# Weight halves moved by 16 to 64 bytes against the other SBUF tensors

## The reference

```python
def _sq_relu_mlp(h, w1, w2):
    a = jax.nn.relu(h @ w1)
    return (a * a) @ w2
```

## Time and profile before

| | us |
|---|---|
| median of 3 runs | 1690.45 |
| lowest and highest | 1687.62, 1692.09 |
| the profiled execution | 1686.52 |
| its span, first to last instruction | 1684.7 |
| TensorE busy | 1643.3 (98%) |
| VectorE busy | 941.8 (56%) |
| ACT busy | 764.6 (45%) |
| POOL busy | 631.6 (37%) |

### The profile page before, as it was taken

One profiled execution on the slowest core, in us unless ns is written; L12 is line 12 of the kernel. 1 busy time (PEld: TensorE's weight loads), 2 busy tenths in 40 slices (PEclk: granted clock), 3 DMA queues, 4 the chain that ended last, 5 costly groups with the idle time before them and its releaser, 6 DMA issues. The chain is left out here.

```text
span 1684.7 us, 26528 instructions
## 1 busy us (share of the span) xinstructions
PE 1643.3 (98%) x10010; PEld 1410.8 (84%) x10010; DVE 941.8 (56%) x1657; ACT 764.6 (45%) x1326; POOL 631.6 (37%) x439
## 2 busy tenths in 40 slices
PE   6999999999999999999999999999999999999998
PEld 4987777788888889989987788798888888989896
DVE  6226566544445249848546664777545576555552
ACT  5324554532223245476545655444445434535351
POOL 1027767342220186643013332965200227323242
PEclk9999999999999999999999999999999999999998
DMA  8322122133333222245632110224411222222221
GB/s 326 128 74 69 56 75 80 54 140 125 120 111 118 100 100 101 101 175 200 238 121 67 51 51 29 97 101 172 178 51 51 101 100 100 101 100 100 100 101 50
DMA packets 29802, 181.68 MB, mean 108 GB/s; under 512 B 3352, under 2 KB 5784, under 8 KB 10112
## 3 DMA queue, kind: packets, MB, share of 16 engines
q1 hardware_dynamic: 22136, 150.12, 24.8%
q10 hardware_dynamic: 7560, 30.09, 5.0%
HBM read 169.57 MB, written 10.50 MB: 107 GB/s over the span
## 5 line engine op out<-in xcount | busy, mean ns | idle before, releaser
L438 PE MATMUL acc<-rarena,wh 128*128 128x512 f32 (+1 forms) x1720 | 650.9, 378 | 6.8 <-ACT farena L1613 1.3
L440 PE MATMUL acc<-rarena,wl 128*128 128x512 f32 (+1 forms) x1720 | 634.6, 369 | 0.0
L439 PE MATMUL acc<-rarena,wh 128*128 128x512 f32 (+1 forms) x1720 | 634.6, 369 | 0.0
L438 PEld LDWEIGHTS acc<-rarena,wh 128*128 128x128 f32 x1720 | 324.1, 188 | 81.3 <-issue 23.5
L440 PEld LDWEIGHTS acc<-rarena,wl 128*128 128x128 f32 x1720 | 324.1, 188 | 55.7
L439 PEld LDWEIGHTS acc<-rarena,wh 128*128 128x128 f32 x1720 | 324.5, 189 | 49.6 <-issue 0.5
L320 DVE TENSOR_TENSOR wl<-raw,wh 128x2048 fp32r<-128x2048 f32 x81 | 198.7, 2453 | 237.2 <-ACT wh L314 237.1
L314 ACT ACTIVATE wh<-raw 128x2048 fp32r<-128x2048 f32 x99 | 188.9, 1908 | 73.1 <-PE acc L440 66.5
L320 POOL TENSOR_TENSOR wl<-raw,wh 128x2048 fp32r<-128x2048 f32 x18 | 82.6, 4588 | 149.3 <-ACT wh L314 149.3
L2555 POOL TENSOR_TENSOR wl<-raw,wh 128x512 fp32r<-128x512 f32 x78 | 104.9, 1372 | 86.6 <-ACT wh L1330 86.4
L516 PE MATMUL acc<-wh,rarena 128*128 128x256 f32 x336 | 95.5, 284 | 2.2 <-DVE rarena L1792 2.1
(11 more groups left out here) (346 smaller groups left out, 3084.0 us busy)
## 6 DMA issues: line engine op xcount, KB each, us to landing
raw<-in_w SPq DMA_DIRECT2D x129, 1024.0 KB, 4.8
early<-in_wmod SPq DMA_DIRECT2D x8, 1024.0 KB, 19.7
farena<-in_gate ACTq DMA_DIRECT2D x4, 1024.0 KB, 4.9
mkv_scratch<-rarena ACTq DMA_DIRECT2D x2, 2048.0 KB, 11.9
rarena<-mkv_scratch ACTq DMA_DIRECT2D x1, 4096.0 KB, 14.4
farena<-in_rpb ACTq DMA_DIRECT2D x16, 240.0 KB, 3.6
farena<-in_x_grid SPq DMA_DIRECT2D x2, 1024.0 KB, 6.3
o_scratch<-early ACTq DMA_DIRECT2D x8, 256.0 KB, 2.0
```

Source lines behind the costliest of these rows:

```text
L438: mm(o, w[0], m[0], start=start, stop=False)
L439: mm(o, w[0], m[1], start=False, stop=False)
L440: return mm(o, w[1], m[0], start=False, stop=stop)
```

## The change

The tensors for the two weight halves become 64 words (256 bytes) longer, and the views on them that the kernel uses start some words in. `phased(name, p0, p1)` places the half for even jobs `p0` bytes and that for odd jobs `p1` bytes from the tensor's start (plus a multiple of 128 for the second). The scratch for DMA descriptors is cut from 16,384 to 64 bytes, which moves every later tensor and makes room. Shapes, order and instructions stay.

```diff
         raw = sb("raw", [128, 2, KT, JW])
-        wh = sb("wh", [128, 2, KT, JW], f32r)
-        wl = sb("wl", [128, 2, KT, JW], f32r)
+        def phased(name, p0, p1):
+            words = ctx.enter_context(nc.sbuf_tensor(name, [128, 2 * KT * JW + 64], f32r))
+            q = KT * JW + (p1 - p0) // 4
+            return words[:, p0 // 4:p0 // 4 + 2 * q].rearrange("p (s q) -> p s q", s=2)[:, :, 0:KT * JW]\
+                .rearrange("p s (k n) -> p s k n", k=KT)
+
+        wh = phased("wh", 16, 32)
+        wl = phased("wl", 48, 64)
...
-    nc = bacc.Bacc("TRN2", target_bir_lowering=False, num_devices=1)
+    nc = bacc.Bacc("TRN2", target_bir_lowering=False, num_devices=1, dynamic_dma_scratch_size=64)
```

## The result

The median of five runs is 1701.92 us (1698.38 to 1704.70) against 1690.41 for the kernel before; the ratio is 1.0075, with a 95% interval from 1.0062 to 1.0088. The forecast was no change.

The account below looks back on a forecast made before the run. The prediction took TensorE's stream of matmuls to bound the kernel; pitch, splits, transfers and scratch each added nothing, 0 us on 1686.5, so a median of 1690 (1687 to 1694 if unchanged), overall range 1665 to 1702.

Parts of the forecast that it names:

- What bounds the kernel: Whole kernel: the stream of matmuls sets the end, TensorE busy 1643.3 of 1684.7 us.
- The pitch: Distance of matmul starts, 226.6 ns at 512 columns and 120.0 at 256; bounds 86 us gained to 23 lost, taken as 0.
- The 13.3 ns: Time of each matmul over its columns, the same at both widths; 6792 matmuls, 90 us in all.
- The first reason: Weights and moving columns slip 3.65 times round 128 bytes per load, so displacement hardly changes how often they meet; 0 us.
- The second reason: 256-column groups average 283 or 284 ns whichever tensors are read, so the 13.3 ns do not depend on that; 0 us.
- The third reason: Other readers and writers of the same tensors, such as DVE, leave no mark on TensorE's steps (227 against 225 ns); 0 us.
- The splits, the transfers, the scratch: Weight splits on ACT and DVE and transfers into raw stay hidden by 6.6 us cover, scratch idle; cost nothing.
- straddling: Slower rival: displaced loads touch five blocks of 128 bytes instead of four, 3.3 ns each, 23 us, 1713; chance 0.11.
- The collision rival: Faster rival: the 13.3 ns are a phase-dependent collision of read streams; one round spared 1666 (0.12), wholly or mostly gone 1604 to 1650 (0.05).

Follow-up runs that it names:

- the control: The changed kernel with all four displacements at 0, scratch still cut and tensors still longer; ratio 0.9998 to the kernel before.
- the map: Kernel of matmul bursts alone, displacement stepped through 256 bytes; with advancing columns none under 226.6 ns at 512 columns, least 113.3 at 256.

## Why the prediction was wrong

- *What bounds the kernel*: right. Of the 13.7 us 13.3 lie in the pitch of the stream of matmuls.
- *The pitch, "between them I take nothing"*: this is the step that failed. The 13.3 ns at 512 columns went to 17.8 and 20.0 in the two kinds of jobs, 4152 matmuls dearer by 4.4 ns on the average (17.5 us over 4010 distances); I had 0. At 256 columns they shrank, by 1.1 ns with weights from the halves and by 1.9 with the halves moving; no case of mine had a loss at one width and a gain at the other.
- *The first reason, the slip of 3.65 rounds*: it counts meetings as if their number made the price. The runs show several settled pitches instead, such as 226.7, 231.1 and 233.3, and 113.3, 117.8 and 120.0. The displacement and the start decide which one, so where the streams meet has a price, whatever the number of meetings.
- *The second reason, equal means whatever is read*: the rows were right and said nothing, since all those groups have the same displacement, 0. I had written that no row shows another phase, and should have left it there.
- *The third reason*: other engines leave no mark, true before and after, but they are not TensorE's own two streams. SBUF — State Buffer of the Trainium skill ("Who interferes with whom") gives TensorE two independent read ports, for moving operand and weights, and I read no change out of that too. The runs do not bear that reading out: in bursts with nothing else at work the places of the two operands change the pitch by 6.7 ns (226.7 to 233.3).
- *The splits, the transfers, the scratch*: right, the control costs nothing (0.9998).
- *The rivals*: straddling had the sign and twice the size (23 us, measured 11.5), but not the cause: the control has every operand off a multiple of 128 and runs as before. The collision rival asked for a gain by any displacement; at 512 columns no place of the map was better than 0 bytes.

What in the chip keeps the rhythm was not settled. Shown is that the time is there when the columns advance through more than four places of 4 bytes, that smaller loads and loads from one place change the pitch without removing the time, and that the displacement and the start pick its value.

## What to carry to other kernels

Where matmuls run back to back, work out the pitch over the columns for each width; if it is the same everywhere, that can be one settled state out of several, and the places of the operands against each other are a setting to measure, per width, in short bursts (here within 256 bytes). A burst must be started in several ways before its number is carried over: one that has two stable pitches can fall on the other in the kernel. And evidence from rows that all share the setting in question is no evidence about changing it.

## What the runs showed of the hardware

- Weights displaced against the columns often cost 6.7 ns a matmul at 512 columns (226.7 to 233.3) and gain up to 6.7 at 256 (120.0 to 113.3), each 16 cycles at 2.4 GHz. Single places of the map are worse: 236.1 at 212 bytes and 512 columns, 122.3 at 108 bytes and 256 columns. In the bursts the displacements 0 and 256 bytes settle alike (226.7, 120.0); 128 does not (233.5 at 512).
- One displacement can have two pitches, and the start picks: 16 bytes at 512 columns had 226.7 in 4 starts and 233.3 in 11.
- An operand whose columns all come from one place runs at 215.7 ns for 512 columns and 111.7 for 256. Reading a window of 16 columns 32 times is slower than reading 512 different ones: 240.0 and 246.7 ns with weights at 0 and 64 bytes.
- Smaller loads don't make a 512-column matmul faster: 226.7, 230.0 and 231.7 ns with 128, 64 and 32 columns of weights. A 256-column matmul they do: 120.0, 113.5 and 113.3.
